# Selection scores of a sparse attention as one-pass products of stacked high and low halves, and the values two steps behind the probabilities

## The reference, cut to what matters

```
s = einsum('bqghd,bngd->bghqn', qb, k_cmp) * scale      # compressed keys: 15 per group
p = masked_softmax(s, valid) * valid
o_cmp = einsum('bghqn,bngd->bqghd', p, v_cmp)
...
s = einsum('bqghd,bgqkd->bghqk', qb, k_g) * scale       # selected blocks (4 blocks, all are selected)
o_sel = einsum('bghqk,bgqkd->bqghd', masked_softmax(s, valid), v_g)
...
s = einsum('bqghd,bkgd->bghqk', qb, k_w) * scale        # window of 512, so all earlier keys
o = gb[..., 0:1] * o_cmp + gb[..., 1:2] * o_sel + gb[..., 2:3] * o_win
```

## Time and profile before

| | |
|---|---|
| time, median of 3 runs | 727.91 us |
| time of the profiled execution | 728.38 us |
| its span, first to last instruction | 726.7 us |
| mean granted clock of TensorE | 0.989 |
| PE busy | 687.4 us (95%) |
| DVE busy | 416.0 us (57%) |
| ACT busy | 395.6 us (54%) |
| mean DMA rate | 150 GB/s |

### The profile page before, as it was taken

How to read it: one execution, slowest core, us unless ns; L and a number is a source line. 1 busy time by engine, 2 the same in 40 slices (tenths; PEclk the granted TensorE clock), 3 DMA queues, 4 the chain that set the end, 5 groups by cost and what they waited for, 6 DMA issues and landing times. The chain is left out here.

```text
span 726.7 us, 9966 instructions
## 1 busy us (share of the span) xinstructions
PE 687.4 (95%) x3553; PEld 575.4 (79%) x3553; DVE 416.0 (57%) x864; ACT 395.6 (54%) x779; POOL 13.2 (2%) x36
## 2 busy tenths in 40 slices
PE   5999899999999999999997998988999999999996
PEld 4888788788778888888886987876878888888885
DVE  4786545787665545444467574455585444444555
ACT  5785647677564443333366486676584333444443
POOL 5000000000000000000000000000000000000000
PEclk9999999999999999999999999998999999999999
DMA  8844305114355555555552344513317554544431
GB/s 306 284 141 129 89 0 175 59 59 123 127 157 175 191 196 204 197 196 189 196 163 63 98 134 146 175 59 116 116 62 235 200 196 175 173 173 173 173 115 58
DMA packets 54480, 108.92 MB, mean 150 GB/s; under 512 B 2272, under 2 KB 16656, under 8 KB 54448
## 3 DMA queue, kind: packets, MB, share of 16 engines
q1 hardware_dynamic: 53536, 105.73, 43.1%
q0 software_dynamic: 912, 2.78, 1.2%
HBM read 107.46 MB, written 1.05 MB: 149 GB/s over the span
## 5 line engine op out<-in xcount | busy, mean ns | idle before, releaser
L281 DVE TENSOR_TENSOR w_lo<-raw,w_hi 128x2048 fp32r<-128x2048 f32 (+6 forms) x111 | 207.8, 1887 | 72.8 <-ACT w_hi L273 72.8
L289 PE MATMUL bank<-w_hi,act_lo 128*128 128x512 f32 (+4 forms) x504 | 198.4, 394 | 5.2 <-DVE w_lo L1878 3.7
L291 PE MATMUL bank<-w_hi,act_hi 128*128 128x512 f32 (+4 forms) x504 | 189.6, 376 | 0.0
L290 PE MATMUL bank<-w_lo,act_hi 128*128 128x512 f32 (+4 forms) x504 | 189.4, 376 | 0.0
L273 ACT ACTIVATE w_hi<-raw 128x2048 fp32r<-128x2048 f32 (+6 forms) x111 | 174.0, 1587 | 9.8 <-PE bank L291 8.7
L289 PEld LDWEIGHTS bank<-w_hi,act_lo 128*128 128x128 f32 x504 | 95.9, 190 | 24.6 <-issue 7.3
L290 PEld LDWEIGHTS bank<-w_lo,act_hi 128*128 128x128 f32 x504 | 96.1, 191 | 17.4 <-issue 1.9
L291 PEld LDWEIGHTS bank<-w_hi,act_hi 128*128 128x128 f32 x504 | 95.8, 190 | 17.1
L1309 ACT ACTIVATE hidT_hi<-bank 128x512 fp32r<-128x512 f32 x20 | 11.9, 597 | 164.0 <-PE bank L774 164.0
L1721 DVE TENSOR_TENSOR hidT_lo<-bank,hidT_hi 128x512 fp32r<-128x512 f32 x20 | 13.8, 692 | 130.1 <-ACT hidT_hi L1309 130.1
L289 PE MATMUL bank<-w_hi,hidT_lo 128*128 128x512 f32 x160 | 63.3, 396 | 0.0
(11 more groups left out here) (214 smaller groups left out, 913.4 us busy)
## 6 DMA issues: line engine op xcount, KB each, us to landing
raw<-in_w_gate_up SPq DMA_DIRECT2D x44, 1024.0 KB, 5.3
raw<-in_w_down SPq DMA_DIRECT2D x22, 1024.0 KB, 4.9
raw<-in_nsa_w_in SPq DMA_DIRECT2D x5, 1024.0 KB, 6.1
raw<-in_w_q_up SPq DMA_DIRECT2D x8, 576.0 KB, 4.0
raw<-in_nsa_w_out SPq DMA_DIRECT2D x4, 1024.0 KB, 5.6
raw<-in_mla_w_out SPq DMA_DIRECT2D x4, 1024.0 KB, 5.2
raw<-in_mla_w_in SPq DMA_DIRECT2D x4, 768.0 KB, 4.6
raw<-in_nsa_w_in SPq DMA_DIRECT2D x6, 384.0 KB, 3.4
```

Source lines behind the costliest of these rows:

```text
L281: ins = dve.tensor_tensor(lo[:, cols], raw[s][:, cols], hi[:, cols].bitcast(F32), ALU.subtract)
L289: pe.matmul(dst, a_lo, b_hi, start=start, stop=False)
L290: pe.matmul(dst, a_hi, b_lo, start=False, stop=False)
L291: return pe.matmul(dst, a_hi, b_hi, start=False, stop=stop)
```

## The change

The diff, cut to what the steps of the argument need:

```diff
+        with nc.sbuf_tensor("k_lo0", [P, QUAD, 2, P], F32R) as k_lo0:
+            pass
+        with nc.sbuf_tensor("pT_third", [P, 512], F32) as pT_third:
...
+        ks_halves = [a.rearrange("p t (i n) -> p t i n", i=2 * QUAD)
+                     for a in (u[:], big[:, 4096:6144].rearrange("p (t n) -> p t n", t=T))]
...
+        probs_at = {"nsa": (pT[:, 0, :], pT[:, 1, :], kc2_[:, 512:1024]), "mla": (pT[:, 0, :], pT[:, 1, :], pT_third[:])}
...
+        def q_halves(to):
+            a = qs_of["nsa"][to % 2].rearrange("p t (i n) -> p t i n", i=QUAD)
+            return a[..., 0:HD], a[..., HD:P]
...
             def scores(m, unit):
...
                 if nsa:
-                    k = kT[0:rows_, turn, :].rearrange("p (b s) -> p b s", b=2)[:, :, 0:keys]
-                    dst = dst.rearrange("p (b s) -> p b s", b=2)
+                    q = queries[m][turn % 2][:, i, t * P:(t + 1) * P]
+                    dst = bank[n % 2][:, 0:2 * keys].rearrange("p (b s) -> p b s", b=2)
+                    pe.matmul(dst, q, k_hi[:, turn, :, 0:keys], start=True, stop=False)
+                    for kt in range(t + 1):
+                        last = pe.matmul(dst[:, :, kt * P:(kt + 1) * P], q, (k_lo0, k_lo1)[kt][:, turn], start=False,
+                                         stop=kt == t)
                 else:
-                    k = mkT[0:rows_, turn % 2, i, 0:keys]
-                pe.matmul(dst, q, k, start=True, stop=True).then_inc(sem(f"{m}_scores"), 1)
+                    last = pe.matmul(bank[n % 2][:, 0:keys], queries[m][turn % 2][0:DK, i, t * P:(t + 1) * P],
+                                     mkT[0:DK, turn % 2, i, 0:keys], start=True, stop=True)
+                last.then_inc(sem(f"{m}_scores"), 1)
...
                     for kt in range(t + 1):
-                        p = pT[:, n % 2, (b * (t + 1) + kt) * P:(b * (t + 1) + kt + 1) * P]
+                        p = probs_at[m][unit % 3][:, (b * (t + 1) + kt) * P:(b * (t + 1) + kt + 1) * P]
...
-                        at_ = t * 64 + i * NCMP
-                        last = pe.matmul(bank[5][:, at_:at_ + NCMP], queries["nsa"][turn % 2][:, i, t * P:(t + 1) * P],
-                                         kcT[:, turn * NCMP:(turn + 1) * NCMP], start=True, stop=True)
+                        at_ = t * P + i * 2 * NCMP
+                        last = pe.matmul(bank[5][:, at_:at_ + 2 * NCMP], queries["nsa"][turn % 2][:, i, t * P:(t + 1) * P],
+                                         kc_halves[:, turn].rearrange("p v n -> p (v n)"), start=True, stop=True)
                 last.then_inc(sem("cmp_scores"), 1)
...
                     fill(n, 1)
-                    if unit > 0:
-                        values(m, unit - 1)
+                    if unit > 1:
+                        values(m, unit - 2)
...
-                        pe.wait_ge(sem("nsa_roped"), turn + 1)
-                    if n < 4:
-                        turn_queries(m, turn, n, turned_at(n))
+            def turn_nsa_queries(turn, n):
+                if n == 0 and turn > 0:
+                    turn_queries("nsa", turn, 3, turned_at(n))
+                if 1 <= n < 4 and turn < TURNS - 1:
+                    if n == 1:
+                        pe.wait_ge(sem("nsa_roped"), turn + 2)
+                    turn_queries("nsa", turn + 1, n - 1, turned_at(n))
...
+            def turn_halves(half):
+                pe.wait_ge(sem("ks_halves"), half + 1)
+                for j in range(2 * T):
+                    b, t = divmod(j, T)
+                    for g in range(QUAD):
+                        last = pe.transpose(K_BANKS[4 * half + j][:, g * P:(g + 1) * P],
+                                            ks_halves[half][:, t, b * QUAD + g, :], ident[:])
+                    last.then_inc(sem("k_turned"), 1)
...
                                    hi[:, cols], lo[:, cols], k == 0, k == KC - 1)
-                    if j == 2 * KC - 1:
-                        last.then_inc(weights_used, 3)
+                    if t == 1 and (c == 2 or k == KC - 1):
...
-            pe.transpose(bank[5][0:HD, 0:CROWS], kcs[0:CROWS, :], ident[0:CROWS, 0:CROWS]).then_inc(sem("kcmp_turned"), 1)
+            for v in range(2):
+                last = pe.transpose(bank[5][:, v * 64:v * 64 + CROWS],
+                                    kcs_halves[:, v].rearrange("p r n -> p (r n)"), ident[0:CROWS, 0:CROWS])
+            last.then_inc(sem("kcmp_turned"), 1)
+            block_values()
...
-                    copy(pT[:, n % 2, 0:width], bank[2 + n % 2][:, 0:width]).then_inc(sem(f"{m}_probsT"), 1)
+                    copy(probs_at[m][(turn * UNITS + n) % 3][:, 0:width], bank[2 + n % 2][:, 0:width]).then_inc(sem(f"{m}_probsT"), 1)
...
                         q_out(m, turn + 2, first + 1)
                     if not nsa and turn < TURNS - 2 and n == 7:
                         kv_out(turn + 2, first + 2)
+                    if nsa and n == 4:
+                        cmp_exp()
                     if turn * UNITS + n + 2 < TURNS * UNITS:
                         exps(m, turn * UNITS + n + 2)
...
                 if m == "nsa":
                     for t in range(T):
                         src = bank[t][:, 0:KVW] if to == 0 else bank[6][:, t * KVW:(t + 1) * KVW]
-                        scaled(qs_of["nsa"][to % 2][:, t, :], src, q_scale(t)) \
+                        src = src.rearrange("p (i n) -> p i n", i=QUAD)
+                        hi, raw_ = q_halves(to)
+                        scaled(raw_[:, t], src, q_scale(t)).then_inc(sem("nsa_q_out"), 1)
+                    for t in range(T):
+                        src = bank[t][:, 0:KVW] if to == 0 else bank[6][:, t * KVW:(t + 1) * KVW]
+                        scaled(hi[:, t].bitcast(F32R), src.rearrange("p (i n) -> p i n", i=QUAD), q_scale(t)) \
                             .then_inc(sem("nsa_q_out"), 1)
...
+            for t in range(T):
+                ins = copy(twice(ks_halves[0][:, t]).bitcast(F32R), to_both(kstage[:, t]))
+            ins.then_inc(sem("ks_halves"), 1)
...
+            def keys_halves_out(half, j):
+                b, t = divmod(j, T)
+                act.wait_ge(sem("k_turned"), 4 * half + j + 1)
+                dst = (k_lo0, k_lo1)[t][:, :, b, :] if half else k_hi[:, :, b, t * P:(t + 1) * P]
+                copy(dst, K_BANKS[4 * half + j][:].rearrange("p (g s) -> p g s", g=QUAD)).then_inc(sem("kT_out"), 1)
...
+                 .rearrange("p v (g n) -> p v g n", g=TURNS)).then_inc(sem("kcT_out"), 1)
+            split_hi(act, NSA_Q1 + 3, 3 * KVW)
+            exps("nsa", 0)
+            exps("nsa", 1)
             q_out("nsa", 1, NSA_Q1 + 2)
             def splits_0(n):
...
             def cmp_masked(turn):
                 dve.wait_ge(sem("cmp_scores"), turn + 1)
-                src = bank[5][:, 0:T * 64].rearrange("p (t n) -> p t n", t=T)[:, :, 0:CROWS]
-                chain.link(dve.tensor_tensor(c4, src.rearrange("p t (i n) -> p t i n", i=QUAD),
-                                             cmask[:].unsqueeze(2).to_broadcast([P, T, QUAD, NCMP]), ALU.add))
+                src = bank[5][:, 0:T * P].rearrange("p (t n) -> p t n", t=T)[:, :, 0:2 * CROWS]
+                src = src.rearrange("p t (i v n) -> p t i v n", i=QUAD, v=2)
+                chain.link(dve.tensor_tensor(c4, src[:, :, :, 0], cmask[:].unsqueeze(2).to_broadcast([P, T, QUAD, NCMP]),
+                                             ALU.add))
+                chain.link(dve.tensor_tensor(c4, src[:, :, :, 1], c4, ALU.add))
...
                         rotate(m, turn + 2)
-                    if n == 7:
+                    if n == (6 if nsa else 7):
                         out_factors(m, turn, 0)
...
+            def q_low(to):
+                hi, lo = (a.rearrange("p t i n -> p (t i) n") for a in q_halves(to))
+                dve.wait_ge(sem("nsa_q_out"), to * 2 * T + 2 * T)
+                chain.link(dve.tensor_copy(hi[:, :, 0:16].bitcast(F32R), lo[:, :, 0:16]))
+                dve.tensor_tensor(lo.bitcast(F32R), lo, hi, ALU.subtract).then_inc(sem("nsa_roped"), 1)
...
+            dve.wait_ge(sem("ks_halves"), 1)
+            for t in range(T):
+                ins = dve.tensor_tensor(twice(ks_halves[1][:, t]).bitcast(F32R), to_both(kstage[:, t]),
+                                        twice(ks_halves[0][:, t]), ALU.subtract)
+            ins.then_inc(sem("ks_halves"), 1)
...
             rotate("nsa", 0)
+            q_low(0)
             split_lo(dve, NSA_Q1 + 2, 2 * KVW)
             masked("nsa", 0)
             masked("nsa", 1)
+            split_lo(dve, NSA_Q1 + 3, 3 * KVW)
```

189 lines of the change are left out of this document (100 added, 89 removed).

## The result

The changed kernel takes 723.17 us (median of six runs, 721.95 to 726.74) against 727.58 for the kernel before, measured beside it: ratio 0.9938, 95% interval 0.9919 to 0.9957, so 4.4 us or 0.6% faster. The forecast was 717.4 us and 10.5 us. The profiled execution took 722.67 us, its span 720.9 us against 726.7.

A forecast was written before the change was run, and what follows sets the result against it. TensorE, busy 95% of the span, was taken as the bound. Its work -11.0, ahead of the turns +0.5, waits in the turns +1.5, layer 1 -1.5 gave -10.5: from 727.9 to 717.4 us, range 707 to 725.

The forecast's parts named there:

- rival 2: Layer 0's turns: ScalarE becomes the bound and half of the 11 us gain is lost to waits, 722.4 us; chance 0.16.
- TensorE's work: Scores 9.2 us less, compressed scores 3.8 less, key transposes 1.9 and 0.1 more: net -11.0 us on TensorE.
- Rival 3: Layer 0's scores: the 48 low-half products run at float32 pace, 14.9 us more, 732.3 us; chance 0.05.
- ahead of the turns: Before layer 0's turns: the wait for rotated second queries grows by about 0.5 us, bounds -1.5 to +3.
- Rival 1: Half-clock stretches at 83.4 us and in layer 1 go, layer 1's waits for probabilities go whole: 711 us; chance 0.17.
- Inside the turns: Layer 0: TensorE loses 3.3 us per turn; waits for exponentials cost 1.5 us over four turns, bounds 0 and 5.
- layer 1: Layer 1's attention: values two steps late save 1.5 of 2.7 us of waits for ScalarE's copied probabilities.
- Rival 4: Layer 0's turns: the clock halves at each turn's start and in turn 3, costing 10 us, 727.5 us; chance 0.05.
- Its sign: For rival 2: ScalarE above 90% in turn 2, with TensorE waiting for exponentials.

The follow-up runs named there:

- e2: The kernel before with only values two steps behind probabilities and a third place for probabilities; 726.70 us, ratio 0.9992.
- e15: Changed kernel, at layer 0's turn borders: first mask ahead of the rotation, compressed product and sum behind the second mask, first output piece one step later; 718.70 us.
- e17: The changed kernel run once more, unaltered; 723.27 us, ratio 0.9945 against the kernel before.
- e1: The changed kernel with values one step behind probabilities again in both layers; 723.06 us, ratio 0.9935.
- e6: The changed kernel without the products of the keys' low halves in the layer 0 scores, 5.8 us of TensorE's work; 722.85 us.
- e11: e9 with the queries' high half made by VectorE and without the products of the keys' low halves in layer 0's scores; 719.82 us.
- e10: e9 with ScalarE's two half splits of output tile 1 moved from steps 3 and 4 of turn 2 to steps 0 and 2; 716.55 us.
- e9: e15 plus, in turn 3, output tile 2's split behind the second piece and, in layer 1, the last two output tiles' splits one step later; 719.08 us.
- e5: The changed kernel with extra TensorE transposes and zero-adding products filling its idle gaps in layer 0's turns; 722.77 us, ratio 0.991.
- e7: The changed kernel with the queries' high half made by a VectorE copy in place of ScalarE's two instructions per query block; 725.86 us.
- e16: e10 with the split of output tile 2 back in step 3 of turn 3, as in the changed kernel; 718.58 us.
- e4: The changed kernel with, at layer 0's turn borders, the rotation behind the first mask and the compressed product and sum behind the second; 723.94 us.
- e13: The changed kernel with only ScalarE's two half splits of output tile 1 moved from steps 3 and 4 of turn 2 to steps 0 and 2; 722.26 us.

## Why the prediction was wrong

The direction came from the part that was right. The size was wrong by more than half: 4.4 us in place of 10.5. The time lies outside the forecast's own band of 712 to 721 us. It is inside the whole range only because that reaches to 725, for rival 2.

**Right: TensorE's work.** The products by `k_hi` and `k_lo` cost what was said:

```profile
136.91 0.39 PE L914 MATMUL bank<-k_hi,q_even 128*128 128x512 f32 x1
137.14 0.40 PE L916 MATMUL bank<-k_lo,q_even 128*128 128x256 f32 x2
137.38 0.60 PE L994 MATMUL bank<-ident,big 128*128 128x128 f32 x4
```

0.23 us from start to start for `k_hi`, 0.24 for the two by `k_lo`. The compressed scores are 32 records in 4.2 us, against 64 before; 3.8 had been said. In the turns 13.0 us less were summed and 10.3 are seen. Counting time at half clock as half (an estimate: 3.4 us of turn 3 after, 1.6 us at 83 us before) it is 12.1. Rival 3 (not one-pass) is out. The second group of transposes of keys:

```profile
62.93 1.97 PE L1096 MATMUL bank<-ident,big 128*128 128x128 f32 x16
64.65 0.39 PE L327 MATMUL bank<-w_hi,act_lo 128*128 128x304 f32 x1
```

16 in 1.97 us with no wait ahead (1.72 to the next start) with 128 columns loaded, where the earlier trace rows has 1.91 with 64. The rule of the Trainium skill that would have added an estimated 2.6 us (TensorE: Matmul & The Clock Gate, section on LDWEIGHTS) does not show as a price here.

**Right: ahead of the turns.** The forecast had +1.9 and +0.1 for transposes and +0.5 for the wait, less the saving of the first five units, 0.19 us for each of four and 0.39 for the fifth: +1.3 at n4. The kernel before has n4 at 90.33, with its stretch at half clock at 83 us in it. e2, with the same scores and without that stretch, has it at 89.37, and the changed kernel at 91.15: +1.8. One execution can't tell this from +1.3: the eleven traces of kernels that are the same up to n4 (the changed one and those that differ from it later) have it from 90.24 to 91.63. That the changed kernel's first execution has no such stretch (others do) gives back up to 1 us to n4 and, by n4 to n6 (7.17 us before, 6.34 in e2), 0.8 behind it. Rival 1 had 1.6 for it.

**Wrong: "Inside the turns" - "I charge 1.5 us for it over the four turns".** This is the step that failed. TensorE's idle time in the attention of layer 0 rose from 4.6 to 9.9 us. 1.4 us of that belong to the term ahead of the turns, and 3.9 stand where 1.5 were charged. The milestones say it without busy times: from n4 to n31 the forecast had 11.9 us less work and 1.5 of friction; measured, and without the two falls of the clock (0.8 us before, 1.0 after), it is 7.0 us less, so the friction is 4.9, at the upper bound of 5. The shares of busy time were forecast well (turn 1: TensorE 20.7, ScalarE 17.9, VectorE 16.6 us, measured 20.79, 17.77 and 16.49), and the friction was taken from them: ScalarE at 17.0 of 20.8 us, VectorE far from full, so waits for exponentials. But the largest waits are for VectorE's masks, 3.4 us, and those for exponentials are 1.1. VectorE's share was never the matter. It works in the order of its program, and at a border of turns that holds a rotation that waits for ScalarE, with the mask behind it. The trace of before had this, with waits of 0.76 us at two borders, and the forecast didn't follow it. e15 moves three things in VectorE's and TensorE's order and is 4.5 us faster by the medians, of the 6 that were missing; 2.45 us of it are seen as pace.

**Right in mechanism, lost elsewhere: layer 1.** Forecast -1.5. By e17 against before, m0 to m31 takes 69.91 us in place of 71.18: -1.3. In the first execution that is hidden by a stretch at half clock at 479 us. Not in the sum was the third unit of values left at the end of layer 0, +0.8 us by the rows above and +1.1 by the milestones. So the lag comes out at nothing, as e1 and e2 have it.

**Rival 2** (ScalarE becomes the bound, half of the gain lost, 722.4 us) was closer than the forecast: it had turn 2 near 19.5 us and turn 1 near 24, and they are 19.79 and 24.16. That TensorE no longer is the bound there is right (e6, e11), and between borders ScalarE's work counts in full (e10 against e9, one pair of splits in turn 2). Its sign, ScalarE above 90% in turn 2, did not come: 16.30 of 19.79 us are 82%. And it had nothing on the borders, where e15 gains without taking work off ScalarE. How the loss divides between the two engines isn't shown. **Rival 4** (the clock; the earlier trace rows has two stretches of the kernel before, its trace has two more, at 387 us and at the very end) was half right, and too high a price at 10 us: the mean clock went from 0.990 to 0.984 and 0.9845, and e15, without the cluster of waits, is back at 0.990. How the 6 us divide between waits and clock can't be given as one number, since a fall costs by its place (below). e5, which has no fall from n6 to n31 and leaves the waits, gets 0.4 us by the medians and about 2 by the ratios. The sentence "I am wrong if PE's work falls by 11 us and the span by less than 4" had the case in view; it was 5.8.

**Left open:** why e10's clock is higher than e9's (the moved split itself gives nothing by milestones), e7's scatter, and what the rotation behind the mask would give to the kernel before.

## What to carry to other kernels

Before cutting the work of the engine that is busy for 95%, list its waits and, for each, what stands ahead of the releasing instruction in its engine's queue, with its own waits: a share of busy time says nothing on that, and the cut lets it surface. Do the reorder together with the cut: the cut alone gives 723.2 us and with the borders reordered 718.7, while on the kernel before the part of the reorder that was tried gives nothing (728.18). The fastest kernel, e10 with 716.55 us, leads e9 by a higher clock, for which no cause is shown. And judge a repair by milestones as well as by the time, since a repair that leaves one wait of 1.8 us may be cancelled by the clock.

## What the runs showed of the hardware

What a stretch at half clock costs differs by its place. By milestones of executions with and without it: 3.4 us at half clock at 84 us cost 0.7 (n4 to n6: 5.29 us, 5.98 in e16), 6.8 at 105 us 1.8 (n10 to n14: 11.71 and in e17 13.50), 6.8 at 129 us 3.1 to 3.6 (e4 against the changed kernel and e15, which differ from it in more than the clock), 6.8 at 154 us 1.0 (n30 to n31: 5.08, in e17 4.04), 3.4 at 479 us 1.5 (m20 to m24: 8.85, in e17 7.34). 6.8 us at 378 us in the gated network cost nothing: e15 takes 269.21 us from n31 to m0 and the first execution of the changed kernel, which has no stretch there, as much. That what bounds the kernel at the place decides the cost is likely and not shown.

In five executions of e13, one program, the spans are 719.5, 720.3, 720.5, 722.8 and 725.4 us at mean clocks of 0.987, 0.984, 0.981, 0.980 and 0.979. So in e13 the time goes with the clock. In others it does less: the fastest of e2's ten has a span of 722.7 us at 0.988, and one at 0.993 has 725.3. The Trainium skill (TensorE: Matmul & The Clock Gate, section on HAM oscillation) puts the falls down to idle gaps between bursts of matmuls. e5 and the pair e4 and e15 agree with that, with gaps shorter than the waits of the section's example: the longest ahead of the fall in e4 is 1.78 us.
